# A two-block transformer on one core: the head of the kernel sends and norms its input tile by tile

## The chip, the core and the metric

The kernel runs on one core of a Trainium2 chip. A core has a matrix engine (PE, with its weight loads PEld), a vector engine (DVE), a scalar engine (ACT), a general engine (POOL) and a sequencer for transfers (SP). Each runs its own instruction stream in order, and they wait for one another on semaphores. ACT and POOL can issue transfers too; all transfers of the core share 16 DMA engines. SBUF is the on-chip memory with 128 partitions, PSUM the memory that PE writes to. The metric is the device time of one execution in microseconds (us), the median of several. Everything is computed in float32.

## The reference, cut to what matters

The model is two blocks over one sequence of 512 tokens with 1024 channels. The first block opens with a norm and a projection, and that opening is what the change is about:

```python
def rms_norm(t, g):
    tf = t.astype(jnp.float32)
    y = tf * lax.rsqrt(jnp.mean(tf * tf, axis=-1, keepdims=True) + NORM_EPS)
    return (y * g.astype(jnp.float32)).astype(t.dtype)

h = rms_norm(x, mix_norm_g[l])          # x: 1 x 512 x 1024
u = h @ w_in[l]                         # 1024 x 2816
conv_in = u[..., :2 * CONV_CH]          # 512 columns: gated depthwise convolution, 31 taps
qkv = u[..., 2 * CONV_CH:]              # 2304 columns: 12 heads, rotary embedding, dilated attention
```

After it come the output projection, an attention over a memory of 256 rows, a mixture of 32 experts of which each token uses two, and a second block (attention with forgetting, a state-space scan, another mixture of experts). None of that is changed.

## The kernel before, in words

The program is written out by hand: one function per stage and engine (`stage1_pe`, `stage1_act`, `stage1_dve`, `stage1_pool`, then `attn1_...`, `mem_pe` and so on), and each engine's block calls its own in order. Nothing reorders the work; the order of the calls and the semaphore waits set it. The sequence is held as four tiles of 128 tokens (`T` = 4), the channels as eight pieces of 128 (`KD` = 8). The matrix multiply needs the channels on the partitions, so `hT[:, k, :]` (piece k of the normed input, all 512 tokens) is made by transposing on PE.

The head goes like this. SP issues the whole of `x` (2 MB) as one transfer (L2692), then seven parameter arrays (`cols`, `rows`, `ident`, `mask1`, `tri`, `tokid`, `posi`, L2693 to L2697) that all count on the semaphore `par_in`, then the weights of the projection in chunks of 512 columns (`load_part`, L318), into a ring of four slots. POOL issues the small transfer `wfv` first of all (L2786): eight columns of a matrix that is 4 KB or more per row, so pieces of 32 bytes, not used until the second block.

DVE fills four areas with constants. ACT and DVE then wait for `x` and for all seven parameter arrays (L488 and L489, L541 and L542), PE for the parameters (L2716). ACT sums the squares of the four tiles (L340), one after another. DVE turns the four sums into four variances with one instruction (L353), POOL raises them to the power -0.5 with one (L368), DVE scales the four tiles (L357). PE transposes 32 squares of 128 x 128 (L376), piece by piece: piece k of all four tiles, so that piece 0 is not complete until the last tile is scaled. ACT and DVE take the eight pieces out of PSUM in turn and apply the gain (L348, L364). Then comes a barrier of the three engines, `end_stage` (L236), a drain and a wait for the three others' drains:

```python
            pe.wait_ge(S("par_in"), 16 * 7)          # L2716
            norm_pe("n1", xn_tile, T)                # L434
            end_stage("pe", pe)                      # L436
```

After it PE runs the projection (L255 through `accumulate`): 16 groups of eight matmuls of 128 x 512, in the order of `FT`. The first four groups use chunk `in0`, the next four `in1`, and so on. Group g from 6 on also waits until group g - 6 has been taken out of PSUM (`g1_out`, L446). While PE runs, DVE computes the angles of the rotary embedding (L546 to L549) from `posi`, ACT clears a table in memory with seven transfers (L495), takes the sine and the cosine (L498, L499) and the sigmoid of the gate (L503), and DVE runs the taps of the convolution.

Of the kernel before, what the change touches and what calls it, by code (L numbers as in the profile page):

```python
# [8 lines left out]
P = 128  # L9
# [6 lines left out]
D = 1024  # L16
# [66 lines left out]
def shared_semaphores():  # L83
# [4 lines left out]
    for tag, tiles in (("n1", 4), ("n4", 2), ("nm", 4), ("n5", 0), ("n6", 0), ("n7", 0), ("n9", 0)):  # L88
        names = (("sumsq", tiles), ("var", 1), ("rstd", 1), ("xn", tiles), ("turned", KD))
        if tag == "n4":  # L90
            names = (("sumsq", MT), ("var", 1), ("rstd", 1), ("xn", MT), ("turned", 4))
# [9 lines left out]
    for tag, n in (("a1", HEADS * T), ("n5", 0), ("x5", MEM_HEADS * T), ("n6", 0), ("n7", 0), ("f2", 8 * T), ("n9", 0)):  # L101
        if not n:
            for what, family, m in (("added", "masked", T if tag == "n7" else 2 * T), ("xa", "probs", T),
                                    ("hd", "pT", T), ("ha", "out", 1 if tag == "n7" else T)):
                shared[f"{tag}_{what}"] = (f"attn_{family}", counts.get(family, 0))
                counts[family] = counts.get(family, 0) + m
            continue
# [9 lines left out]
    shared["x5_max"] = ("a1_sq", HEADS // 2)  # L117

# [36 lines left out]
def recycled_semaphores():  # L155
# [8 lines left out]
               "halves_set", "x_in", "mem_in", "sp_ra", "sp_sin", "x5_max", "x5_norm")  # L164
# [8 lines left out]
def build(nc, a, out):  # L173
    es = ExitStack()
    with es:
# [13 lines left out]
        def since(name):  # L189

            return SHARED.get(name, (name, 0))[1]
# [116 lines left out]
        def load_part(sp, part):  # L308
            for i, (nm, w, c0, c1) in enumerate(chunks):
# [177 lines left out]
        def stage1_act(act):  # L487
            act.wait_ge(S("x_in"), 16)  # L488
            act.wait_ge(S("par_in"), 16 * 7)  # L489
            norm_act("n1", x_tile, D, T, hT_tile, gains("mix_g"))  # L490
            end_stage("act", act)
# [5 lines left out]
            act.wait_ge(S("angles"), 1)  # L497
            nc.scalar.activation(sin_t, sin_t, ACT.Sin)  # L498
# [33 lines left out]
        def stage1_dve(dve):  # L532
# [92 lines left out]
        def stage1_pool(pool):  # L625
            pool.wait_ge(S("halves_set"), 1)
            norm_pool("n1", T)
# [377 lines left out]
        def s5_matrices_pool(pool):  # L1005
# [11 lines left out]
            after_stage(pool, 3)  # L1017
# [1054 lines left out]
        STAGES_TO_MOE1 = 2 + 1 + 1 + 2  # L2072
# [34 lines left out]
        def entry_act(act):  # L2107
# [11 lines left out]
            for t in range(T):  # L2119
                act.wait_ge(S(f"xback_{t}"), 16)  # L2120
# [14 lines left out]
        def entry_dve(dve):  # L2135
# [4 lines left out]
            def gained(t):  # L2140
                dve.wait_ge(S(f"xback_{t}"), 16)
                dve.tensor_tensor(x[:, t, :], xn[:, t, :], final_g, ALU.mult).then_inc(S("n7_added"), 1)
# [642 lines left out]
        def _(pool):  # L2785
            pool.dma_start(wfv, a["w_in_2"][0][:, 1536:1544].rearrange("(k p) n -> p k n", p=P)).then_inc(S("wf_in"), 16)  # L2786
# [110 lines left out]
```

## Time and profile before

| | |
|---|---|
| median of 3 runs | 1939.67 us (1931.63 to 1944.18) |
| profiled execution, its own time | 1940.19 us |
| its span | 1938.3 us |
| PE busy | 1657.2 us, 85% of the span |
| DVE, ACT, POOL busy | 503.6, 327.0, 375.5 us |
| chain that ended last | PE 54%, DMA 29%, DVE 6%, POOL 4%, ACT 3% |
| mean granted PE clock of the span | 0.944 of full speed |
| time at which the projection's first matmul starts | 35.50 us |

The page divides the span into 40 slices, so the first slice (48 us) holds the whole head: PE is busy half of it, and DMA moves 285 GB/s. Everything finer has to be asked of the trace: the chain of waits in a window of the first 64 us, the transfers with the time from issue to landing, and the busy time and bytes moved by stretch. Two readings need care. A landing is counted from the issue of a transfer, so it holds the time behind earlier transfers in the queue. And the granted clock of the first stretches is printed as 1.00, though the first change that the trace records comes only when PE has run for some us; a matmul's own duration says more there.

### The profile page before, as it was taken

Reading aid. Unit: us, or ns where it says so; the run is one execution under the profiler, and the core shown is the slowest. Engines: PE = TensorE matmul, PEld = TensorE weight load, DVE = VectorE, ACT = ScalarE, POOL = GpSimd, SP = SyncE. Lnnn points to the kernel's source line nnn. Section 1 sums busy time; section 2 is a strip of 40 time slices with the busy share of each in tenths; the row PEclk is TensorE's granted clock in tenths of the full one; section 3 lists DMA queues with packets and bytes.
Section 4 is the critical chain, followed back from the end, with each engine's and each line's share of the span. In section 5 each row is a group of like instructions: output and inputs, shape, how many; then the busy total and the mean of one; then the engine's idle time right before and its main releaser. Section 6 shows DMA issues by size and latency. Waiting matters only on the chain.

```text
span 1938.3 us, 18659 instructions
## 1 busy us (share of the span) xinstructions
PE 1657.2 (85%) x7098; PEld 809.9 (42%) x7098; DVE 503.6 (26%) x1200; ACT 327.0 (17%) x705; POOL 375.5 (19%) x357
## 2 busy tenths in 40 slices
PE   4999889989897988777787759899999997988775
PEld 2444447434545332322222225545644444544332
DVE  3466666020315210100000021613300015311110
ACT  2001552020412000000000020313400012111111
POOL 0011552974011011111111110010001001232222
PEclk9999999989997999999999969999999997999998
DMA  8112103430653999999999854940031235999992
GB/s 285 65 44 87 66 1 130 160 112 22 226 200 143 412 414 420 419 417 418 417 419 416 314 204 113 256 107 33 1 78 56 84 156 223 402 398 404 402 398 96
DMA packets 101670, 436.96 MB, mean 225 GB/s; under 512 B 15608, under 2 KB 23448, under 8 KB 75344
## 3 DMA queue, kind: packets, MB, share of 16 engines
q1 hardware_dynamic: 59136, 299.22, 40.6%
q10 hardware_dynamic: 23984, 105.80, 13.3%
q0 software_dynamic: 18464, 30.76, 6.0%
q8 instruction: 58, 0.95, 0.2%
q14 instruction: 28, 0.23, 0.0%
HBM read 414.19 MB, written 40.91 MB: 235 GB/s over the span
## 4 chain that ended last, share of the span: by engine, by line
PE 54%; DMA 29%; DVE 6%; POOL 4%; ACT 3%; issue 3%; SPq 1%; ACTq 0%; POOLq 0%; DVEq 0%
PE ps L255 27%; DMA ring<-in_w 18%; PE ps L1711 8%; DMA ring<-in_w_expert_up 7%; PE ps L1294 5%; DMA work<-hmid,rowtok 2%; PE ps L1727 2%; PE ps L2192 2%; PE ps L721 1%; PE ps L706 1%; PE ps L1320 1%; PE ps L680 1%; DMA ring<-in_positions 1%; POOL ring L1054 1%; POOL ring L1055 1%
## 5 line engine op out<-in xcount | busy, mean ns | idle before, releaser
L1711 PE MATMUL ps<-ring,work 128*64 128x256 f32 (+1 forms) x1472 | 273.8, 530 | 75.0 <-DMA ring<-in_w 41.6
L255 PE MATMUL ps<-kept,ring 128*128 128x512 f32 x640 | 280.7, 598 | 2.5 <-DVE kept L1349 1.3
L1711 PEld LDWEIGHTS ps<-ring,work 128*64 128x64 f32 x1472 | 113.2, 150 | 239.4 <-issue 120.1
L255 PEld LDWEIGHTS ps<-kept,ring 128*128 128x128 f32 x640 | 122.2, 192 | 156.6 <-issue 154.0
L1829 DVE TENSOR_TENSOR work<-work,ps 128x256 f32<-128x256 f32 (+1 forms) x64 | 22.7, 355 | 627.5 <-ACT work L1788 606.8
L1727 PE MATMUL ps<-ring,work 128*64 128x512 f32 x544 | 129.3, 610 | 27.2 <-issue 26.2
L1711 PE MATMUL ps<-kept,work 128*64 128x512 f32 (+1 forms) x640 | 120.1, 533 | 28.4 <-DMA kept<-in_w 17.9
L1875 POOL DMA_INDIRECT hres<-work,rowdst x33 | 51.7, 1567 | 433.6 <-ACT work L1798 433.3
L255 PE MATMUL ps<-ring,kept 128*128 128x512 f32 (+1 forms) x320 | 124.7, 550 | 0.3 <-PE ps L255 0.3
L1294 PE MATMUL ps<-ring,kept 128*128 128x512 f32 x256 | 114.8, 603 | 1.7 <-ACTq L239 1.4
L1788 ACT ACTIVATE work<-ps 128x256 f32<-128x256 f32 (+1 forms) x64 | 21.2, 331 | 456.9 <-PE ps L1711 456.9
L1711 PEld LDWEIGHTS ps<-kept,work 128*64 128x64 f32 x640 | 50.2, 150 | 100.5 <-issue 52.8
L1875 POOL DMA_INDIRECT out<-work,rowdst x33 | 51.7, 1568 | 192.5 <-ACT work L1798 191.3
L255 PEld LDWEIGHTS ps<-ring,kept 128*128 128x128 f32 x320 | 60.5, 190 | 62.5 <-issue 60.9
L1798 ACT ACTIVATE work<-ps,gslot 128x512 f32<-128x512 f32 x64 | 44.0, 687 | 244.0 <-PE ps L1727 244.0
L1727 PEld LDWEIGHTS ps<-ring,work 128*64 128x64 f32 x544 | 40.5, 139 | 84.1 <-issue 82.8
L1294 PEld LDWEIGHTS ps<-ring,kept 128*128 128x128 f32 x256 | 48.4, 193 | 61.0 <-issue 58.0
L255 PE MATMUL ps<-work,ring 128*128 128x128 f32 (+2 forms) x416 | 66.7, 310 | 1.5 <-DVEq L239 0.5
L1727 PE MATMUL ps<-kept,work 128*64 128x512 f32 x240 | 55.9, 599 | 11.2 <-issue 11.2
L255 PEld LDWEIGHTS ps<-work,ring 128*128 128x128 f32 x416 | 58.9, 191 | 7.4 <-DVE ring L2596 2.3
L1294 PE MATMUL ps<-ring,work 128*128 128x512 f32 x128 | 56.9, 596 | 2.4 <-POOL work L2681 2.2
L2681 POOL TENSOR_TENSOR work<-work 128x512 f32<-128x512 f32 x8 | 10.1, 1261 | 234.7 <-DVE work L2674 234.7
(449 smaller groups left out, 1877.3 us busy)
## 6 DMA issues: line engine op xcount, KB each, us to landing
ring<-in_w SPq DMA_DIRECT2D x46, 2048.0 KB, 30.3
kept<-in_w SPq DMA_DIRECT2D x21, 2048.0 KB, 30.1
ring<-in_w ACTq DMA_DIRECT2D x20, 2048.0 KB, 22.6
ring<-in_w_in SPq DMA_DIRECT2D x13, 2048.0 KB, 14.8
ring<-in_w_expert_gate SPq DMA_DIRECT2D x24, 1024.0 KB, 33.8
ring<-in_w_expert_up SPq DMA_DIRECT2D x24, 1024.0 KB, 40.5
kept<-in_w ACTq DMA_DIRECT2D x9, 2048.0 KB, 25.6
ring<-in_w_expert_down ACTq DMA_DIRECT2D x18, 1024.0 KB, 29.2
```

Of the source, the lines that this page charges most:

```text
L255: last = nc.tensor.matmul(out_, l, r, start=i == 0, stop=i == len(pairs) - 1)
L680: nc.tensor.matmul(ps[:, (i + m) % 4, :], q1[r, h // 2, t * P:t * P + P], k1[r, h // 2, :], start=True, stop=True).then_inc(S("a1_scores"), 1)
L706: last = nc.tensor.transpose(ps[:, 4 + j % 2, c * P:c * P + P], pr1(j)[:, c * P:c * P + P], ident[:, :])
L721: last = nc.tensor.matmul(ps[64 * m:64 * m + 64, 6, :], v1[:, c, (2 * hp + m) * 64:(2 * hp + m) * 64 + 64], pT1(hp)[:, m, c, :], start=c = ...
L1294: last = nc.tensor.matmul(ps[:, b * T + t, :], src(k)[:, t * P:t * P + P], weight(nm)[:, k, :], start=k == 0, stop=k == KD - 1)
L1711: last = nc.tensor.matmul(ps[64 * hf:64 * hf + 64, bank, 0:ff].rearrange("p (w n) -> p w n", w=2), xT[:, k, :], up[:, :, k * ff + hf * hw: ...
L1727: last = nc.tensor.matmul(ps[64 * hf:64 * hf + 64, bank, :], hT_[:, i % nch, 64 * (i // nch):64 * (i // nch) + 64], down[:, i, hf * 512:hf ...
L1788: nc.scalar.activation(gb[:, i % 2, 0:hw], ps[:, i % 2, 0:hw], ACT.Silu).then_inc(S(f"silu{m}"), 1)
L1798: nc.scalar.activation(yb[:, j % 4, :], ps[:, 6 + j % 2, :], ACT.Identity, scale=gslot[:, expert(j):expert(j) + 1]).then_inc(S(f"yready{m} ...
L1829: dve.tensor_tensor(hb[:, i % 2, 0:hw], gb[:, i % 2, 0:hw], ps[:, i % 2, hw:ff], ALU.mult).then_inc(S(f"hready{m}"), 1)
L1875: return pool.indirect_dma_start(out=by_half(acc(m)), out_offset=bass.IndirectOffsetOnAxis(ap=rows_, axis=0), in_=src, in_offset=None, bou ...
L2192: last = nc.tensor.matmul(ps[64 * q:64 * q + 64, s2, :], hs[:, k, 2 * s2 + q, :], weight("u")[:, k, :], start=k == 0, stop=k == KD - 1)
```

## The change

The diff is cut to what the instructions do. What is left out renumbers barriers (one fewer ahead of every later one) and semaphores that are used again later, and moves no work.

```diff
 block.sync:
-            sp.dma_start(x[:, :, :], a["x"][0].rearrange("(t p) n -> p t n", p=P)).then_inc(S("x_in"), 16)
-            for dst, src in ((cols[:, :], a["cols"]), (rows[:, :], a["rows"].to_broadcast([P, NROW])),
-                             (ident[:, :], a["ident"]), (mask1[:, :], a["mask1"]),
-                             (tri[:, :], a["tri"]), (tokid[:, :], a["tokid"]),
-                             (posi[:, :], a["positions"].unsqueeze(0).to_broadcast([P, SEQ]))):
-                sp.dma_start(dst, src).then_inc(S("par_in"), 16)
+            for t in range(T):
+                sp.dma_start(x[:, t, :], a["x"][0, t * P:t * P + P, :]).then_inc(S(f"x_tile_{t}"), 16)
             load_part(sp, False)
 load_part:
+                if i == 1:
+                    for dst, src in ((posi[:, :], a["positions"].unsqueeze(0).to_broadcast([P, SEQ])),
+                                     (rows[:, :], a["rows"].to_broadcast([P, NROW])), (mask1[:, :], a["mask1"]),
+                                     (tri[:, :], a["tri"]), (tokid[:, :], a["tokid"])):
+                        sp.dma_start(dst, src).then_inc(S("par_in"), 16)
 stage1_pe:
-            norm_pe("n1", xn_tile, T)
-
-            end_stage("pe", pe)
+            for t in range(T):
+                pe.wait_ge(S("n1_xn"), since("n1_xn") + t + 1)
+                for k in range(KD):
+                    last = nc.tensor.transpose(ps[:, 2 * t + k // 4, (k % 4) * P:(k % 4) * P + P],
+                                               xn[:, t, k * P:k * P + P], ident[:, :])
+                last.then_inc(S("n1_turned"), 1)
+            pe.wait_ge(S("n1_hd"), since("n1_hd") + T)
+            pe.wait_ge(S("n1_ha"), since("n1_ha") + T)
 stage1_act:
-            act.wait_ge(S("x_in"), 16)
-            act.wait_ge(S("par_in"), 16 * 7)
-            norm_act("n1", x_tile, D, T, hT_tile, gains("mix_g"))
-            end_stage("act", act)
+            act.dma_start(cols[:, :], a["cols"]).then_inc(S("id_in"), 16)
+            act.dma_start(ident[:, :], a["ident"]).then_inc(S("id_in"), 16)
+            act.wait_ge(S("halves_set"), 1)
+            nc.scalar.activation(nmax[:, 0:16], halves[:, :], ACT.Square)
+            for t in range(T):
+                act.wait_ge(S(f"x_tile_{t}"), 16)
+                if t >= 2:
+                    act.wait_ge(S("n1_sumsq"), since("n1_sumsq") + t - 1)
+                nc.scalar.activation(junk[:, :] if t % 2 else junk2[:, 0:D], x[:, t, :], ACT.Square,
+                                     accum_out=st[:, t:t + 1]).then_inc(S("n1_sumsq"), 1)
+            act.wait_ge(S("id_in"), 32)
+            for t in range(T):
+                act.wait_ge(S("n1_turned"), since("n1_turned") + t + 1)
+                for k in range(4, KD):
+                    last = nc.scalar.activation(hT[:, k, t * P:t * P + P], ps[:, 2 * t + 1, (k - 4) * P:(k - 3) * P],
+                                                ACT.Identity, scale=col("mix_g", k))
+                last.then_inc(S("n1_ha"), 1)
 ...
             act.wait_ge(S("angles"), 1)
+            act.wait_ge(S("par_in"), 16 * 5)
 stage1_dve:
-            dve.wait_ge(S("x_in"), 16)
-            dve.wait_ge(S("par_in"), 16 * 7)
-            norm_dve("n1", x_tile, D, T, xn_tile, hT_tile, gains("mix_g"))
-            end_stage("dve", dve)
-
+            def scaled(t):
+                dve.wait_ge(S(f"x_tile_{t}"), 16)
+                dve.wait_ge(S("n1_sumsq"), since("n1_sumsq") + t + 1)
+                dve.tensor_scalar(st[:, 8 + t:9 + t], st[:, t:t + 1], 1.0 / D, EPS, ALU.mult, ALU.add).then_inc(
+                    S("n1_var"), 1)
+                dve.wait_ge(S("n1_rstd"), since("n1_rstd") + t + 1)
+                dve.tensor_scalar(xn[:, t, :], x[:, t, :], st[:, 16 + t:17 + t], None, ALU.mult).then_inc(S("n1_xn"), 1)
+
+            def turned(t):
+                dve.wait_ge(S("n1_turned"), since("n1_turned") + t + 1)
+                dve.tensor_tensor(hT[:, 0:4, t * P:t * P + P], ps[:, 2 * t, :].rearrange("p (k s) -> p k s", k=4),
+                                  col("mix_g", 0, 4).unsqueeze(2).to_broadcast([P, 4, P]), ALU.mult).then_inc(S("n1_hd"), 1)
+
+            scaled(0)
+            scaled(1)
+            dve.wait_ge(S("id_in"), 32)
+            for t in range(2, T):
+                scaled(t)
+                turned(t - 2)
+            for t in range(T - 2, T):
+                turned(t)
+
+            dve.wait_ge(S("par_in"), 16 * 5)
 stage1_pool and block.gpsimd:
-            pool.dma_start(wfv, ...).then_inc(S("wf_in"), 16)     (was ahead of stage1_pool)
-            norm_pool("n1", T)
+            for t in range(T):
+                pool.wait_ge(S("n1_var"), since("n1_var") + t + 1)
+                nc.gpsimd.tensor_tensor(st[:, 16 + t:17 + t], st[:, 8 + t:9 + t], halves[:, 0:1], ALU.pow).then_inc(
+                    S("n1_rstd"), 1)
+            pool.dma_start(wfv, ...).then_inc(S("wf_in"), 16)
 block.tensor:
-            pe.wait_ge(S("par_in"), 16 * 7)
+            pe.wait_ge(S("id_in"), 32)
             stage1_pe(pe)
+            pe.wait_ge(S("par_in"), 16 * 5)
```

How this moves instructions shows at three places. The first is SP's queue at the start of the program (`kept<-in_x` is the input, `ring<-in_w_in` the chunks of the projection, `ring<-in_mask` the array `mask1`). Before:

```order
L2692 DMA kept<-in_x 128x4x1024
L2697 DMA cols<-in_cols 128x247
L2697 DMA rows<-in_rows 128x844
L2697 DMA ident<-in_ident 128x128
L2697 DMA ring<-in_mask 128x896
L2697 DMA tri<-in_tri 128x128
L2697 DMA tokid<-in_tokid 128x4
L2697 DMA ring<-in_positions 128x512
L318 DMA ring<-in_w_in 128x8x512 x5
```

and with the change:

```order
L2745 DMA kept<-in_x 128x1024 x4
L329 DMA ring<-in_w_in 128x8x512
L325 DMA ring<-in_positions 128x512
L325 DMA rows<-in_rows 128x844
L325 DMA ring<-in_mask 128x896
L325 DMA tri<-in_tri 128x128
L325 DMA tokid<-in_tokid 128x4
L329 DMA ring<-in_w_in 128x8x512 x4
```

The input is four transfers, the first chunk of weights stands ahead of the parameters, and `cols` and `ident` have gone to ACT's queue. The second place is DVE at the same point (`kept` holds `x`, `xn` and `hT`; `st` the sums, variances and factors). Before:

```order
L539 MEMSET work 128x1024
L353 TENSOR_SCALAR st<-st 128x4
L357 TENSOR_SCALAR kept<-kept,st 128x1024 x4
L364 TENSOR_SCALAR kept<-ps,cols 128x512 x4
L546 CAST kept<-ring 128x512
```

and with the change:

```order
L569 MEMSET work 128x1024
L574 TENSOR_SCALAR st<-st 128x1
L577 TENSOR_SCALAR kept<-kept,st 128x1024
L574 TENSOR_SCALAR st<-st 128x1
L577 TENSOR_SCALAR kept<-kept,st 128x1024
L574 TENSOR_SCALAR st<-st 128x1
L577 TENSOR_SCALAR kept<-kept,st 128x1024
L581 TENSOR_TENSOR kept<-ps,cols 128x4x128
L574 TENSOR_SCALAR st<-st 128x1
L577 TENSOR_SCALAR kept<-kept,st 128x1024
L581 TENSOR_TENSOR kept<-ps,cols 128x4x128 x3
L594 CAST kept<-ring 128x512
```

The variance and the scaling now alternate tile by tile, and the first tile is taken out of PSUM before the last is scaled. The third is ACT. Before:

```order
L340 ACT_TABLE_LOAD
L340 ACTIVATE junk,st<-kept 128x1024 x4
L348 ACTIVATE kept<-ps,cols 128x512 x4
L492 DMA kept<-in_perm 128x128
L495 DMA ssm_t<-work 512x1x32
```

and with the change:

```order
L504 DMA cols<-in_cols 128x247
L505 DMA ident<-in_ident 128x128
L507 ACT_TABLE_LOAD
L507 ACTIVATE nmax<-halves 128x16
L512 ACTIVATE ring,st<-kept 128x1024
L512 ACTIVATE junk,st<-kept 128x1024
L512 ACTIVATE ring,st<-kept 128x1024
L512 ACTIVATE junk,st<-kept 128x1024
L518 ACTIVATE kept<-ps,cols 128x128 x16
L521 DMA kept<-in_perm 128x128
```

Two transfers, the table load and a small activation stand ahead of the first square, and sixteen activations of 128 columns take the place of four of 512.

## Rows read from the trace of the kernel before

**Rows 1.** Chain of waits, 0 to 64 us: start, duration (us), what it was.
```profile
4.79 13.91 DMA ring<-in_positions
...
18.78 1.28 ACT L340
...
23.61 1.16 ACT junk L340 x2
...
26.32 2.75 DVE kept L357 x4
...
35.50 27.75 PE ps L255 x64
```

**Rows 2.** Transfers, 0 to 130 us: issuer, count, KB each, us from issue to landing.
```profile
kept<-in_x SPq DMA_DIRECT2D x1, 2048.0 KB, 14.2
...
ring<-in_positions SPq DMA_DIRECT2D x1, 256.0 KB, 13.9
...
kept<-in_perm ACTq DMA_DIRECT2D x1, 64.0 KB, 4.9
...
wf<-in_w_in POOLq DMA_DIRECT2D x1, 32.0 KB, 12.1
```

**Rows 3.** POOL's queue, 5 to 13 us: packets, MB, share of the 16 DMA engines.
```profile
q0 software_dynamic: 30, 0.03, 43.5%
```

**Rows 4.** Timeline of the issuing queues; then landings of the first and second weight chunk.
```profile
1.29 1.12 POOL L2786 DMA_DIRECT2D wf<-in_w_in  x1 [0.87 <-POOLq L2890]
...
7.48 7.92 SPq L318 DMA_DIRECT2D ring<-in_w_in  x2
...
ring<-in_w_in SPq DMA_DIRECT2D x1, 2048.0 KB, 16.6
...
10.18 5.22 SPq L318 DMA_DIRECT2D ring<-in_w_in  x1
ring<-in_w_in SPq DMA_DIRECT2D x1, 2048.0 KB, 19.4
```

**Rows 5.** Busy time by stretch; the last three columns are granted clock, DMA share, GB/s.
```profile
0.00:4.00 4.00, 0.00 (x0) 0.00 (x0) 2.22 (x4) 0.00 (x0) 1.31 (x5) 1.00 0.49 130
4.00:6.00 2.00, 0.00 (x0) 0.00 (x0) 0.75 (x1) 0.00 (x0) 0.00 (x0) 1.00 1.06 417
7.00:13.00 6.00, 0.00 (x0) 0.00 (x0) 0.00 (x0) 0.00 (x0) 0.00 (x0) 1.00 0.55 189
15.00:20.00 5.00, 0.00 (x0) 0.00 (x0) 0.00 (x0) 1.22 (x1) 0.00 (x0) 1.00 1.05 393
```

**Rows 6.** Chain of waits, 420 to 495 us: a later norm, last tile.
```profile
425.97 0.22 DVE st L1434
...
426.26 0.56 POOL st L1399
...
427.76 1.11 PE ps L1320 x8
...
428.89 0.70 DVE kept L1349
...
430.13 30.77 PE ps L255 x64
...
461.04 27.72 PE ps L255 x64
```

**Rows 7.** Chain at 395 to 410 us; two stretches with PE busy, and the clock.
```profile
403.33 1.97 PE ps L1320 x8
...
429.50:436.50 7.00, 6.37 (x8) 2.74 (x9) 0.08 (x1) 0.54 (x3) 6.69 (x6) 0.52 0.33 124
606.00:638.00 32.00, 20.41 (x110) 15.31 (x112) 14.41 (x58) 4.69 (x10) 4.46 (x5) 0.52 0.58 211
```

**Rows 8.** Timeline, 399 to 400 us: POOL and DVE side by side.
```profile
399.49 3.50 POOL L1065 MEMSET ring<- 128x4096 f32 x1
...
399.56 3.71 DVE L1338 TENSOR_SCALAR kept<-kept,st 128x512 f32<-128x512 f32 x1 [3.43 <-POOL st L1399]
```

More of the change, by code:

```diff
@@ L89, in shared_semaphores @@
         names = (("sumsq", tiles), ("var", 1), ("rstd", 1), ("xn", tiles), ("turned", KD))
+        if tag == "n1":
+            names = (("sumsq", T), ("var", T), ("rstd", T), ("xn", T), ("turned", T))
         if tag == "n4":
@@ L100, in shared_semaphores @@
     counts = {}
-    for tag, n in (("a1", HEADS * T), ("n5", 0), ("x5", MEM_HEADS * T), ("n6", 0), ("n7", 0), ("f2", 8 * T), ("n9", 0)):
+    for tag, n in (("n1", 0), ("a1", HEADS * T), ("n5", 0), ("x5", MEM_HEADS * T), ("n6", 0), ("n7", 0), ("f2", 8 * T), ("n9", 0)):
         if not n:
@@ L104, in shared_semaphores @@
                                     ("hd", "pT", T), ("ha", "out", 1 if tag == "n7" else T)):
+                if tag == "n1" and what in ("added", "xa"):
+                    continue
                 shared[f"{tag}_{what}"] = (f"attn_{family}", counts.get(family, 0))
@@ L117, in shared_semaphores @@
     shared["x5_max"] = ("a1_sq", HEADS // 2)
+    for t in range(T):
+        shared[f"xback_{t}"] = (f"x_tile_{t}", 16)
     for family, tags in (("sum", (("g1", 24), ("m4", 12), ("r3", 8), ("q5", 8), ("r5", 8), ("u", 4), ("glu", 4),
@@ L163, in recycled_semaphores @@
                "ctok_in", "ln_done", "ln_sig", "angles", "ln_var", "ln_rstd", "sines", "perm_in", "zeros", "zeroed",
-               "halves_set", "x_in", "mem_in", "sp_ra", "sp_sin", "x5_max", "x5_norm")
+               "halves_set", "id_in", "mem_in", "sp_ra", "sp_sin", "x5_max", "x5_norm")
     assert len(later) == len(earlier)
@@ L626, in stage1_pool @@
             pool.wait_ge(S("halves_set"), 1)
-            norm_pool("n1", T)
+            for t in range(T):
+                pool.wait_ge(S("n1_var"), since("n1_var") + t + 1)
+                nc.gpsimd.tensor_tensor(st[:, 16 + t:17 + t], st[:, 8 + t:9 + t], halves[:, 0:1], ALU.pow).then_inc(
+                    S("n1_rstd"), 1)
+            pool.dma_start(wfv, a["w_in_2"][0][:, 1536:1544].rearrange("(k p) n -> p k n", p=P)).then_inc(S("wf_in"), 16)
             for f in range(12):
@@ L1016, in s5_matrices_pool @@
             halves = (slice(0, 64), slice(64, P))
-            after_stage(pool, 3)
+            after_stage(pool, 2)
             pool.dma_start(raw_bc, a["ssm_bc"]).then_inc(S("bc_in"), 16)
@@ L2069, in over_sp @@
                                      ).then_inc(S(f"over{m}_down_{p}"), 16)
-        STAGES_TO_MOE1 = 2 + 1 + 1 + 2
+        STAGES_TO_MOE1 = 1 + 1 + 1 + 2
         sp_ = lambda at, *shape: (lambda v: v if len(shape) == 1 else v.rearrange("p (a b) -> p a b", a=shape[0]))(
@@ L2119, in entry_act @@
             for t in range(T):
-                act.wait_ge(S(f"xback_{t}"), 16)
+                act.wait_ge(S(f"xback_{t}"), since(f"xback_{t}") + 16)
                 square(t, xn[:, t, :], 2 * t)
@@ L2140, in gained @@
             def gained(t):
-                dve.wait_ge(S(f"xback_{t}"), 16)
+                dve.wait_ge(S(f"xback_{t}"), since(f"xback_{t}") + 16)
                 dve.tensor_tensor(x[:, t, :], xn[:, t, :], final_g, ALU.mult).then_inc(S("n7_added"), 1)
@@ L2691, in _ @@
         def _(sp):
-            sp.dma_start(x[:, :, :], a["x"][0].rearrange("(t p) n -> p t n", p=P)).then_inc(S("x_in"), 16)
-            for dst, src in ((cols[:, :], a["cols"]), (rows[:, :], a["rows"].to_broadcast([P, NROW])),
-                             (ident[:, :], a["ident"]), (mask1[:, :], a["mask1"]),
-                             (tri[:, :], a["tri"]), (tokid[:, :], a["tokid"]),
-                             (posi[:, :], a["positions"].unsqueeze(0).to_broadcast([P, SEQ]))):
-                sp.dma_start(dst, src).then_inc(S("par_in"), 16)
+            for t in range(T):
+                sp.dma_start(x[:, t, :], a["x"][0, t * P:t * P + P, :]).then_inc(S(f"x_tile_{t}"), 16)
             load_part(sp, False)
@@ L2785, in _ @@
         def _(pool):
-            pool.dma_start(wfv, a["w_in_2"][0][:, 1536:1544].rearrange("(k p) n -> p k n", p=P)).then_inc(S("wf_in"), 16)
             stage1_pool(pool)
```

## The prediction

> **What bounds the kernel now.** I began with the chain of waits over the first 64 us, because the change touches nothing behind it. The reader is to see two halves in [rows 1]. Up to 18.7 us nothing is computed on the path: all engines wait for `posi`, the last of the transfers issued ahead of the weights. From 18.78 to 35.50 us a chain of 16.7 us follows that PE mostly only ends: table load, four squares of 1.16 us, variance, power, four scalings in 2.75 us, 32 transposes, two evictions, barrier. At 35.50 PE starts on 64 matmuls without a gap, and the same chain stays on PE from there through the projection. So the head is worth 35.50 us, and what the change can save is what it takes off that number, if PE finds its weights and runs as fast as now.
>
> Next the transfers. Input and parameters are only 3.3 MB, 8 to 9 us at the rate of 393 to 417 GB/s that the steady stretches show [rows 5], yet `x` lands at 0.72 + 14.2 = 14.9 us and `posi` at 4.79 + 13.9 = 18.7 us [rows 2]. Between them lies a stretch of 6 us at 189 GB/s in which the engines are charged only 0.55 of their time [rows 5]. The row that stands out beside it is POOL's queue: 0.03 MB that hold 43.5% of 16 engines over 8 us, 3.5 us on each engine [rows 3]. That is `wfv`, 32-byte pieces, issued at 1.29 us and landed 12.1 us later [rows 2, 4]. I read the slow stretch as its doing: `x` is being sent at 417 GB/s until it comes [rows 5], and finishes only after it.
>
> The Trainium skill, page "DMA: Bandwidth & Descriptors", section "Queues, rings and completion order", says that a DMA engine takes turns between queues packet by packet and finishes a packet before it switches. By that rule every packet of `x` behind a slow one of `wfv` waits for it whole, and moving `wfv` frees `x`; the trace agrees in the 3.5 us per engine [rows 3].
>
> **The change, part by part.** 1. *First tile.* 130 GB/s over 4 us is 0.52 MB, exactly one tile, by 4.0 us [rows 5]. `cols` and `ident` (0.19 MB) now run on ACT's queue beside it, 0.45 us at 417 GB/s, and the landing follows the last byte: I take 4.8 us. Upper end: the 64 KB of `perm` took 4.9 us beside a full stream [rows 2]; with that from an issue at 0.72, and 1.1 us for the other 0.46 MB, 6.7 us. Lower end 4.0.
>
> The same page, section "Anatomy of one DMA — SWDGE (gpsimd) path", gives a fixed cost of about 2.0 us per transfer and 436 GB/s; an estimate from it is 0.72 + 2.0 + 1.2 = 3.9 us for the first tile. By that estimate the sum would be 0.9 us better; no row here shows such a transfer alone.
>
> 2. *The chain per tile.* A later norm of this kernel is already built tile by tile and gives the prices: variance 0.22 us, power of one column 0.56, 0.07 between the two [rows 6]. The scaling is 2.75 / 4 = 0.69 [rows 1]. With the gaps that is 1.6 us per tile, all in series on DVE, which waits for POOL in between. First square done at 4.8 + 1.16, seen by DVE at 6.1. Three tiles: 10.9. Then one eviction, 0.70 [rows 6]: 11.6. Fourth tile: 13.2. Its eight transposes: 1.97 us at half clock, against 1.11 at full [rows 6, 7]: 15.2. From the start of the last DVE eviction to PE's first matmul the later norm takes 430.13 - 428.89 = 1.24 us, ACT's four small activations included [rows 6]: **16.5 us**. The other two evictions of DVE fit under the transposes.
>
> 3. *Covers.* ACT's four squares end at 4.8 + 4 x 1.2 = 9.6, before DVE wants the last at 11.6; the table load (1.28 us [rows 1]) now lies ahead of the first tile. The last tile needs 2.29 MB: 0.52 by 4.0, the rest in 4.2 us, so 8.2, landed about 8.9; it is wanted at 10.3. Without that cover every us later is a us lost. `cols` and `ident` are wanted at 9.3 and come by about 1.7 + 4.9 = 6.6. The first weights: 4.39 MB, 0.52 by 4.0 and 3.87 at 393 GB/s, so 13.9, landed about 14.6, 2 us before PE wants them.
>
> 4. *Barrier removed.* It stood between the last eviction and PE; in the 1.24 there is none, so nothing is added.
>
> 5. *PE's clock.* In the old head the first 64 matmuls took 27.75 us, as long as 64 in a settled stretch (27.72): the transposes had run in one block before them [rows 1, 6]. Now the transposes come in four bursts with gaps. The nearest row is the later norm, also in bursts: its next 64 matmuls took 30.77, **3.05 us** more, with a granted clock of 0.52, that is 1.2 GHz, over 429.5 to 436.5 [rows 6, 7]. I charge that; the other end is nothing.
>
> 6. *`wfv` moved.* POOL issues it after the fourth power, about 12.6 us, beside DVE's last scaling. Where POOL filled memory beside a scaling, that scaling took 3.71 us instead of 0.69 [rows 8]. The issue takes 1.12 us [rows 4], so 0 to 1.1 us; I take 0, the middle of what the two rows allow being well under the other terms. The transfer itself now runs into the second weight chunk. PE wants that one half of 27.75 after its start, plus the slow clock: 33 us. It landed at 10.18 + 19.4 = 29.6 us [rows 4] with the same bytes and `wfv` ahead of it. ACT's clearing of memory (1.8 MB, 4.6 us at 393) now comes early enough to push it at worst to 34. I charge nothing; the end is 1 us.
>
> 7. *Parameters behind the weights.* 1.2 MB more in the queue behind 13.9 us, so landed at about 18, 1.5 us after PE's start. DVE's angles, ACT's sine and sigmoid hang on them; PE asks for the sigmoid first in group 6, 6 x 27.75 / 8 = 20.8 us after its start, and in the old head never waited for it, since its 64 matmuls ran through [rows 1]. Nothing; if the slack there was under 1.5 us, the rest of it.
>
> Sum: 35.5 - 16.5 = 19.0 saved at the start of PE, less 3.05, is 15.95. From there on every wait is on PE or on a transfer that PE's progress releases, so the shift should reach the end whole. The profiled execution was 1940.19 us, 0.5 above the median: 1924.2, which I give as **1924 us**.
>
> **Rivals.** *A, the input still comes late.* If the slow stretch is not the doing of `wfv` but of so many transfers at once, the last tile lands at 14.9. Then 1.16 + 0.15 for the square, 1.6 for the chain, 1.97 and 1.24: PE at 21.0, saving 14.5 - 3.05 = 11.4, 1928.8 us. For it: engines idle in that stretch, which blocked packets alone do not explain. Against it: the 417 GB/s before. Chance 0.17.
>
> *B, PE keeps full clock.* Nothing is lost at the start: 1921.2 us. For it: 32 transposes in 8 us are PE work too. Against it: [rows 7]. Chance 0.20.
>
> *C, the clock stays low.* With PE busy 64% of 606 to 638 us the granted clock was 0.52 throughout [rows 7]. If the bursts leave PE at 1.2 GHz into the projection, each us at that level loses half of it: the change decides to the bad from 2 x 19.0 = 38 us at half clock. All first 64 matmuls so would take 55.5 us, a loss of 27.75: 1949 us. Against it: busy without gaps, PE came back within 7 us in [rows 6, 7]. Chance 0.03.
>
> *D, the shift is lost on the way.* Some later stage starts by something that PE does not set, and the end stays: 1938 to 1941 us. For it: DMA has 29% of the whole chain. Against it: every such load waits for a slot that PE frees. Chance 0.08.
>
> The forecast has 0.52. **Numbers.** The runs before spread over 12.6 us, so a median of a few is good to some 4 us; 1% is 19.4 us and about what can be told from no change. Faster by over 1% means below 1920.3: near half of B, a fifth of the forecast for noise and for unpriced luck: 0.24. Slower by over 1%: C beyond its point and what nobody thought of: 0.03. Within: 0.73. The range must hold 8 in 10: the forecast's own is 1919 to 1930 (terms 1, 5, 6 and noise); it takes in A and B with noise: 1915 to 1932.
>
> **What the profile after would show.** The first matmul of 128x512 at 16 to 18 us (A: 21). Landings of the four tiles at about 5, 6, 8, 9. POOL's powers at 0.56 each. The first 64 matmuls at 30 to 31 us (B: under 28). No wait of PE for a weight chunk in the first 200 us. The attention's start earlier by as much as the projection's. Wrong would be: DVE waiting for `cols`, PE waiting for chunk two, or a power of 1.05 us per tile instead of 0.56, which would cost 4 x 0.5 = 2 us.

## The result and the profile after

The changed kernel takes 1912.93 us (median of 4, 1910.08 to 1920.20), the kernel before 1936.47 (median of 4, the three shown and one more). The ratio is 0.9882, 95% interval 0.9856 to 0.9908: faster by 1.2%. The forecast was 1924 us with a range of 1915 to 1932: the direction is right, and the time lies 2 us below the range. The profiled execution took 1914.55 us, 25.64 less than the one of before; the part of this that the head explains is 20.3 us, as shown below.

The chain of waits over the first 64 us of the changed kernel, in the columns of [rows 1]:

```profile
0.72 4.07 DMA kept<-in_x
...
4.81 1.16 ACT ring L512 x2
...
6.08 0.17 DVE st L574
...
6.39 0.58 POOL st L677
...
7.00 0.76 DVE kept L577
...
7.90 4.92 PE ps L448 x24
...
12.84 1.76 ACT kept L518 x6
...
15.21 27.72 PE ps L261 x64
```

What PE waited for last is in its row of the timeline:

```profile
15.21 9.25 PE L261 MATMUL ps<-kept,ring 128*128 128x512 f32 x21 [1.28 <-ACT kept L518]
```

It is ACT's four small activations for the last tile, which end at 15.1 us; DVE's last eviction ends at 14.7.

The first tile is there at 4.79 us, PE transposes from 7.90, and the first 128x512 matmul is at 15.21 instead of 35.50. The 64 matmuls take 27.72 us, as before (27.75), and end at 42.93 instead of 63.25: 20.3 us earlier. The stretch that was slow before [rows 3, 5] is gone:

```profile
7.00:13.00 6.00, 5.06 (x25) 4.86 (x26) 4.01 (x9) 5.11 (x15) 2.65 (x4) 1.00 1.04 395
```

395 GB/s where it was 189, and PE, DVE and ACT are busy in it. The transfers, in the columns of [rows 2] (the first row is the fourth tile, issued at 2.10 us, the second the first chunk of weights, issued at 2.72):

```profile
kept<-in_x SPq DMA_DIRECT2D x1, 512.0 KB, 6.8
ring<-in_w_in SPq DMA_DIRECT2D x1, 2048.0 KB, 11.6
cols<-in_cols ACTq DMA_DIRECT2D x1, 123.5 KB, 4.3
wf<-in_w_in POOLq DMA_DIRECT2D x1, 32.0 KB, 13.0
```

So the last tile lands at 8.9 us and the first chunk at 14.3, close to what was worked out (8.9 and 14.6). The chunk is now 0.9 us ahead of PE and no more.

Behind the head the two profiles drift apart by 5 us. The starts of some groups of PE in both, from the trace:

| PE's group | before, us | after, us | earlier by |
|---|---|---|---|
| first scores of the attention (L680, now L732) | 201.2 | 181.0 | 20.2 |
| transposes of the memory (L689, now L741) | 293.0 | 272.7 | 20.3 |
| projection behind the memory (L1294, now L1346) | 359.3 | 340.6 | 18.7 |
| router of the first block (L1286, now L1338) | 589.3 | 568.2 | 21.1 |
| state-space part (L2340, now L2392) | 1234.9 | 1213.3 | 21.6 |
| last matmul of the last experts (L1727, now L1779) | 1923.6 | 1897.9 | 25.7 |

It goes down as well as up. The granted clock is at half for 215.2 us in all in the one trace and for 200.7 in the other, added up from the clock's records within the span (the expectation below has both 1.6 us higher). Up to the router of the first block the steps stand where one execution has such a stretch and the other has not. The twelve profiles of this study that run the whole computation show it: from the first scores to the transposes of the memory they take 91.7 to 92.0 us where 6.8 us of it are at half, 88.9 or 89.0 where none are, and 93.2 in the one with 10.2. From there to the projection it is 67.9 or 68.0 us with 3.4 us at half and 66.2 or 66.3 with none. The last step, 4.1 us in the last stretch of the table, is not explained in this way. That stretch takes 684.3 to 688.9 us over the twelve profiles, in no clear order with its time at half clock, and the cause of the step stays open.

### The profile page after: what moved, and what is told of

Read it like the earlier page. It is cut to its first block, busy times and chain, and to the rows that moved or that the text cites. A ratio compares the mean times of both kernels' runs of the same rounds, so it can differ in the third digit from the quotient of the medians.

```text
span 1912.7 us, 18683 instructions
## 1 busy us (share of the span) xinstructions
PE 1652.7 (86%) x7098; PEld 807.8 (42%) x7098; DVE 503.5 (26%) x1203; ACT 328.6 (17%) x718; POOL 376.9 (20%) x360
## 3 DMA queue, kind: packets, MB, share of 16 engines
q10 hardware_dynamic: 24272, 105.99, 13.5%
## 4 chain that ended last, share of the span: by engine, by line
PE 53%; DMA 30%; DVE 7%; POOL 4%; ACT 3%; issue 2%; SPq 1%; ACTq 0%; POOLq 0%; DVEq 0%
PE ps L261 27%; DMA ring<-in_w 19%; DMA ring<-in_w_expert_up 9%; PE ps L1763 8%; PE ps L1346 5%; PE ps L1779 2%; PE ps L2244 2%; DMA work<-hmid,rowtok 1%; PE ps L773 1%; PE ps L758 1%; SPq L1942 1%; PE ps L1372 1%; PE ps L732 1%; POOL ring L1106 1%; POOL ring L1107 1%
## 5 line engine op out<-in xcount | busy, mean ns | idle before, releaser
L1779 PE MATMUL ps<-ring,work 128*64 128x512 f32 x544 | 129.5, 611 | 27.2 <-issue 26.2
L1346 PE MATMUL ps<-ring,kept 128*128 128x512 f32 x256 | 114.5, 602 | 1.7 <-ACTq L245 1.4
L1840 ACT ACTIVATE work<-ps 128x256 f32<-128x256 f32 (+1 forms) x64 | 21.1, 330 | 458.4 <-PE ps L1763 458.4
L1779 PEld LDWEIGHTS ps<-ring,work 128*64 128x64 f32 x544 | 40.5, 139 | 84.1 <-issue 82.7
L1346 PEld LDWEIGHTS ps<-ring,kept 128*128 128x128 f32 x256 | 48.2, 193 | 60.9 <-issue 57.8
L1779 PE MATMUL ps<-kept,work 128*64 128x512 f32 x240 | 55.9, 599 | 11.2 <-issue 11.2
L1346 PE MATMUL ps<-ring,work 128*128 128x512 f32 x128 | 56.9, 596 | 2.4 <-POOL work L2733 2.2
L2733 POOL TENSOR_TENSOR work<-work 128x512 f32<-128x512 f32 x8 | 10.1, 1261 | 234.7 <-DVE work L2726 234.7
## 6 DMA issues: line engine op xcount, KB each, us to landing
kept<-in_w ACTq DMA_DIRECT2D x9, 2048.0 KB, 25.6
```

What stands on the lines that cost most here:

```text
L1346: last = nc.tensor.matmul(ps[:, b * T + t, :], src(k)[:, t * P:t * P + P], weight(nm)[:, k, :], start=k == 0, stop=k == KD - 1)
L1779: last = nc.tensor.matmul(ps[64 * hf:64 * hf + 64, bank, :], hT_[:, i % nch, 64 * (i // nch):64 * (i // nch) + 64], down[:, i, hf * 512:hf ...
L1840: nc.scalar.activation(gb[:, i % 2, 0:hw], ps[:, i % 2, 0:hw], ACT.Silu).then_inc(S(f"silu{m}"), 1)
```

## The experiments

Ratios are to runs of the kernel before on the same chip, made in the same session. "The end of the 64" is the end of the first 64 matmuls of the projection: it holds both when PE starts and how fast it runs, and it is 63.25 us in the profile of before and 42.93 in the changed one.

### The same kernels again

The changed kernel with no edit:

> The changed kernel once more, timed against the one before in five rounds. Theory 'head plus luck': in the two profiles PE starts the projection 20.3 us earlier and the end comes 25.6 us earlier; the last 5 us arise later, at places where PE's granted clock is at half in one execution and not in the other (216.8 us at half clock before, 202.3 after). Then a new profile again has its first 128x512 matmul at 15.2 us to within 0.2, but another span, and the span goes with the granted clock; over more runs the difference of the medians falls towards 20 us (ratio 0.9895). Rival 'the later stages gain too': the difference stays at 23.5 us or more and the new profile shows the same steps at the same places as the first.

Measured: 0.9906, interval 0.9888 to 0.9924, median 1917.85 of 6 runs, against 1936.51 for 17 runs of before. Its profile:

```profile
0.72 4.25 DMA kept<-in_x
...
13.03 1.11 PE ps L448 x8
...
15.39 27.72 PE ps L261 x64
```

The head repeats within 0.2 us (15.39 against 15.21). The later steps do not: PE starts the projection behind the memory at 336.3 us, 23.0 earlier than in the first profile of before, where the first changed profile had 18.7. So the rival, the same steps at the same places, fell for this part. Its six runs reach from 1912.62 us at a mean granted clock of 0.946 to 1921.89 at 0.942, while the profiled run of 1913.1 us has 0.950. 0.9906 of 1936.5 is a saving of 18.2 us, with 14.7 to 21.7 in the interval; the head's 20.3 lies inside, the 25.6 of the first pair of profiles does not.

The kernel before with no edit:

> The kernel before against itself, for the spread that the executions have of their own and for a second profile of it. Theory: the head repeats to within 0.3 us (first 128x512 matmul at 35.5), while the span differs by some us, with the sum of the stretches at half clock; the ratio is 1.000 with an interval of about 0.2% to each side. Rival: the span repeats to within 1 us, and then the 5 us that the changed kernel's profile gained behind the head were no chance.

Measured: 1.000, interval 0.9986 to 1.0015, median 1936.99. Its ten runs reach from 1930.62 us (clock 0.950) to 1940.48 (clock 0.943). The head does not repeat as closely as I expected: the chain has

```profile
4.31 14.83 DMA ring<-in_positions
...
36.49 23.87 PE ps L255 x55
```

one us later than in the first profile, since the parameters land at 19.1 us instead of 18.7 and the transposes take 6.08 us instead of 5.52. Medians of before over four sets of runs were 1936.5, 1936.5, 1934.3 and 1936.6; the 1939.67 of the section ahead of the prediction was 3 us high, and the 1940.19 from which the forecast was counted 3.7 us.

### The transfer of 32-byte pieces

The changed kernel with `wfv` first again:

```diff
 stage1_pool:
-            pool.dma_start(wfv, ...).then_inc(S("wf_in"), 16)
 block.gpsimd:
+            pool.dma_start(wfv, ...).then_inc(S("wf_in"), 16)
             stage1_pool(pool)
```

> The changed kernel with one line moved back: POOL issues the transfer of 32-byte pieces (wfv) first of all. Theory: its slow packets fall among those of x again; between about 7 and 13 us the rate drops from 395 GB/s to about 200, the last tile lands at 12 to 15 us instead of 8.9, PE starts the projection at 18 to 21 us instead of 15.2, and the run is 3 to 6 us slower than the changed kernel. Rival (A of the prediction): the slow stretch came from many small transfers at once, which are no longer ahead; then x lands by 9 us as now, and nothing moves by more than 1 us.

Measured: 0.9939, interval 0.9919 to 0.9959, so 8 us slower than the changed kernel by the medians (1925.98 against 1917.85), more than expected. In its chain, its stretches and POOL's queue at 5 to 13 us:

```profile
1.63 14.48 DMA kept<-in_x
...
21.12 1.98 PE ps L448 x8
...
24.36 29.74 PE ps L261 x64
```

```profile
7.00:13.00 6.00, 3.64 (x16) 3.28 (x16) 1.54 (x3) 0.43 (x2) 0.55 (x1) 1.00 0.47 174
15.00:28.70 13.70, 8.27 (x22) 5.08 (x23) 6.91 (x14) 6.62 (x20) 1.10 (x2) 0.51 1.02 375
```

```profile
q0 software_dynamic: 28, 0.03, 50.5%
```

The rate falls to 174 GB/s, the third tile lands at 16.1 us, the fourth at 17.2, and PE starts 9.2 us later. It also starts slower: 29.74 us for the 64 and a clock of 0.51 over 15.0 to 28.7. (The DMA engines are busy for 0.47 of the slow stretch, and for 0.55 of it in the kernel before; why they stand idle for the rest stays open.) The end of the 64 is at 54.10, 11.2 us later. One transfer of 32 KB costs half of what the whole change gains.

The kernel before with this line alone moved, behind the power of the norm:

```diff
 block.gpsimd:
-            pool.dma_start(wfv, ...).then_inc(S("wf_in"), 16)
 stage1_pool:
             norm_pool("n1", T)
+            pool.dma_start(wfv, ...).then_inc(S("wf_in"), 16)
```

> The kernel before with the same one line moved only: wfv is issued behind the power, at about 26 us. Theory: no slow stretch at 7 to 13 us; x, parameters (3.3 MB) land by 10 to 12 us instead of 18.7, all later steps of the head follow unchanged (16.7 us), PE starts at 27 to 29 us instead of 35.5, and the time falls by 7 to 8 us. Rival: the parameters themselves are slow to send (512-byte to 3.5 KB rows, eight transfers); they still land at 16 us or later and the time falls by under 3 us.

Measured: 0.9967, interval 0.9954 to 0.9980, a saving of 6.4 us (3.9 to 8.9).

```profile
4.49 9.04 DMA ring<-in_positions
...
24.26 6.16 PE ps L376 x29
...
31.28 27.75 PE ps L255 x64
```

```profile
kept<-in_x SPq DMA_DIRECT2D x1, 2048.0 KB, 7.9
```

`x` lands at 8.6 us instead of 14.9, `posi` at 13.5 instead of 18.7, and PE starts 4.2 us earlier, at 31.28 and not at the 27 to 29 expected. Neither theory holds whole: the slow stretch was the doing of `wfv`, but the parameters took longer than their bytes (13.5 where I had 10 to 12; 319 GB/s over 10 to 13.5 us). And of the 5.2 us by which they land earlier PE keeps 4.2, since the four scalings take 3.07 us here instead of 2.75 and the transposes 6.16 instead of 5.52.

Is it the pieces, or that POOL issues a transfer there? The changed kernel with POOL sending `cols` first, rows of 988 bytes:

```diff
 stage1_act:
-            act.dma_start(cols[:, :], a["cols"]).then_inc(S("id_in"), 16)
 block.gpsimd:
+            pool.dma_start(cols[:, :], a["cols"]).then_inc(S("cols_in"), 16)
             stage1_pool(pool)
 ...
```

The dots stand for the waits of ACT, DVE and PE, which go over to `cols_in`.

> The changed kernel, with POOL sending the array cols (rows of 988 bytes, 124 KB) first of all instead of ACT; wfv stays behind the powers. It asks what of wfv slowed x: its pieces of 32 bytes, or that POOL issued a transfer at this time. Theory: the pieces; the rate at 7 to 13 us stays near 395 GB/s, x lands by 9 us, and PE starts at 15 to 16 us unless cols itself lands after 9 us. Rival: POOL's queue; the rate falls to about 200 GB/s and x lands at 12 us or later.

Measured: one run, 1913.46 us. One stretch, the landing of `cols`, and the chain:

```profile
7.00:13.00 6.00, 4.63 (x28) 4.42 (x29) 4.01 (x9) 5.37 (x17) 2.92 (x4) 1.00 1.04 390
```

```profile
cols<-in_cols POOLq DMA_DIRECT2D x1, 123.5 KB, 5.2
```

```profile
14.94 27.72 PE ps L261 x64
```

Four times the bytes from the same queue at the same moment, and 390 GB/s. So it is not that POOL issues a transfer there but how that transfer is cut: 1024 pieces of 32 bytes, spread over the rows of a matrix, against 128 rows of 988. Which of these, size, number or spacing, does it is not told apart.

### The order of the transfers, and the norm by tiles

The parameters ahead of the first chunk of weights:

```diff
-                if i == 1:
+                if i == 0:
                     for dst, src in ((posi[:, :], ...), (rows[:, :], ...), ...
```

> The changed kernel with the five parameter arrays sent ahead of the first chunk of weights instead of behind it. Theory: 1.2 MB ahead of the chunk at 390 to 400 GB/s are 3 us, so the chunk lands at 17 to 17.5 us instead of 14.3 and PE, ready at 15.2, starts 2 us later. Rival: small rows are sent more slowly than their bytes say; the chunk lands at 19 us or later.

Measured: one run, 1924.69 us.

```profile
5.29 14.62 DMA ring<-in_w_in
20.05 29.64 PE ps L261 x64
```

The chunk lands at 19.9 us, 5.6 later and not 3, and PE starts at 20.05. After its wait the 64 matmuls take 29.64 us. Two stretches and POOL's queue at 13 to 20 us say where the other 2.6 us went:

```profile
7.00:10.00 3.00, 2.10 (x10) 2.13 (x11) 1.67 (x5) 2.69 (x6) 1.10 (x2) 1.00 1.04 330
...
16.00:20.00 4.00, 0.00 (x0) 0.00 (x0) 3.78 (x7) 0.00 (x0) 0.00 (x0) 0.64 1.24 278
```

```profile
q0 software_dynamic: 27, 0.03, 25.7%
```

The parameters go at 330 GB/s instead of 393 to 417, and behind them the chunk, now late, meets `wfv`, which holds 1.8 us of every engine there.

`x` as one transfer:

```diff
-            for t in range(T):
-                sp.dma_start(x[:, t, :], a["x"][0, t * P:t * P + P, :]).then_inc(S(f"x_tile_{t}"), 16)
+            sp.dma_start(x[:, :, :], a["x"][0].rearrange("(t p) n -> p t n", p=P)).then_inc(S("x_tile_0"), 16)
 ...
```

(The dots: ACT and DVE wait for `x_tile_0` alone.)

> The changed kernel with x as one transfer of 2 MB instead of four; all engines wait for the whole of it. Theory: it lands at 8 to 9 us (the last tile lands at 8.9 now), the four squares follow at 1.2 us each, the last one's variance, power, scaling, transposes and evictions take 4.5 us more, and PE starts at 17.5 to 18 us, 2.5 us later than the changed kernel. Rival: four transfers cost the queue something that one does not; x lands by 7.5 us and the loss is under 1.5 us.

Measured: one run, 1917.11 us.

```profile
0.72 8.39 DMA kept<-in_x
...
19.54 27.72 PE ps L261 x64
```

It lands at 9.1 us, where the four tiles are done at 8.9, so four transfers cost the queue nothing. PE starts at 19.54, 4.3 later and not 2.5: all four steps of DVE and POOL now run behind the landing at 1.5 us each, and not only the last.

The changed transfers with the norm of before in one piece, and no barrier:

```diff
 stage1_dve:
+            dve.tensor_scalar(st[:, 8:8 + T], st[:, 0:T], 1.0 / D, EPS, ALU.mult, ALU.add).then_inc(S("n1_var"), 1)
+            dve.wait_ge(S("n1_rstd"), since("n1_rstd") + 1)
+            for t in range(T):
+                dve.tensor_scalar(xn[:, t, :], x[:, t, :], st[:, 16 + t:17 + t], None, ALU.mult).then_inc(S("n1_xn"), 1)
+ ...
+            for k in range(1, KD, 2):
+                dve.wait_ge(S("n1_turned"), since("n1_turned") + k + 1)
+                dve.tensor_scalar(hT[:, k, :], ps[:, k, :], col("mix_g", k), None, ALU.mult).then_inc(S("n1_hd"), 1)
```

> The changed kernel's transfers, table load and missing barrier, but the norm itself as before: one variance for four tiles, one power, four scalings, transposes piece by piece, evictions piece by piece. Theory: the tile-wise chain is a part of the gain of its own. The four squares still end at 10.1 us; from there the old chain took 35.50 - 24.77 = 10.7 us with the barrier, so PE starts the projection at 20.5 to 21 us, 5.5 us later than the changed kernel, with its 64 matmuls at 27.7 us, and the time is 5 to 6 us above the changed kernel's. Rival: the transfers are the whole gain and the order of the norm is covered by the landing of the first weights (14.3 us); then PE starts by 17 us.

Measured: 0.9945, interval 0.9928 to 0.9962, median 1922.46 of 7 runs.

```profile
2.10 6.86 DMA kept<-in_x
...
8.98 1.16 ACT junk L507 x2
...
10.49 1.06 POOL st L379
11.58 3.07 DVE kept L582 x4
14.70 5.21 PE ps L387 x29
19.93 0.76 DVE kept L586
20.74 27.75 PE ps L261 x64
```

PE starts at 20.74, as expected: the norm by tiles is worth 5.5 us of the 20.3, and the transfers, the table load and the missing barrier together the other 14.8. The two chains say how that divides: what all wait for lands at 8.96 us instead of 18.70, which is 9.7 us; one square stands behind it instead of the table load and four squares, 4.9 us; and from the last square to PE it takes 10.6 us against 10.7, so the barrier was worth next to nothing (0.05 us between DVE's last eviction and PE, where the kernel before has 0.08).

DVE scaling the last tile ahead of the first eviction:

```diff
-            for t in range(2, T):
-                scaled(t)
-                turned(t - 2)
-            for t in range(T - 2, T):
-                turned(t)
+            scaled(2)
+            scaled(3)
+            for t in range(T):
+                turned(t)
```

> The changed kernel with DVE scaling the last tile ahead of the first eviction. DVE's eviction of tile 0 (0.68 us) stands in the way of the last variance, whose square is there 1.1 us earlier. Theory: the last scaling ends 0.6 us earlier and PE starts the projection at 14.6 to 14.9 us instead of 15.2. Rival: the evictions pile up behind it, or the first weights (landed at 14.3 us) set the start; 15.0 us or later.

Measured: one run, 1917.65 us.

```profile
11.64 2.21 ACT kept L518 x8
14.36 0.53 ACT kept L518 x2
14.98 27.72 PE ps L261 x64
```

It gains 0.23 us, not 0.6: what PE waits for last are ACT's evictions, here as in the changed kernel, and an earlier scaling on DVE helps those little. It is no version to prefer, since a quarter of a us cannot be told from none. No kernel of this study is measurably faster than the changed one.

### PE's clock at the start of the projection

24 of the 32 transposes left out. The evictions of those three tiles read `x` itself instead (behind the dots), so ACT and DVE have the same work; what follows the head works on other data, and only the head is read:

```diff
 stage1_pe:
                 pe.wait_ge(S("n1_xn"), since("n1_xn") + t + 1)
+                if t < T - 1:
+                    pe.sem_inc(S("n1_turned"), 1)
+                    continue
                 for k in range(KD):
 ...
```

> Part of the computation changes: the transposes of tiles 0 to 2 are left out, PE only signals, and their evictions read x untransposed; all else stands, so DVE and ACT do the same work and PE has 8 transposes ahead of the projection instead of 32. What follows has other data (another routing), so only the head is read. Theory on the clock: what PE did in the 7 us ahead of the first matmul decides; with 8 transposes the first 64 matmuls of 128x512 take 30 to 31 us, with a granted clock at half for some us after about 15 us, where with 32 they took 27.7. Rival: the clock at the start has nothing to do with the transposes (it is up at that time anyway); the 64 matmuls take 27.7 us again.

Measured, in the head of one profile:

```profile
12.74 1.98 PE ps L451 x8
...
15.99 29.36 PE ps L261 x64
```

With PE idle until 12.74 the eight transposes take 1.98 us, where the changed kernel's last eight take 1.11, and the 64 matmuls 29.36 where they take 27.72. The trace's first record of the clock, a rise to full, is at 19.30 us; up to it the matmuls start 0.85 us apart, which is 1.2 GHz, and behind it 0.43. In the changed kernel that record is at 12.21 us, among the transposes: they start 0.21 us apart before it and 0.11 after. So the transposes are what brings the clock up in time, and the theory holds; the price is 1.6 us, below the 2.3 to 3.3 that I expected.

How soon the clock rises differs between executions. In six profiles with these 32 transposes ahead the record comes at 10.48, 11.02, 11.87, 12.21, 13.68 and 13.77 us, each time before PE could start the projection (14.94 us at the earliest).

PE made to wait ahead of the projection:

```diff
             pe.wait_ge(S("n1_ha"), since("n1_ha") + T)
+            pe.wait_ge(S("par_in"), 16 * 5)
             used = 0
```

> The changed kernel, but PE waits ahead of the projection for the five parameter arrays, which land at 22.9 us, so that it stands idle for 9 us after its 32 transposes. Theory on the clock: the idle time costs again what the transposes gained; PE starts at 23.0 us and the first 64 matmuls take 29.5 to 31 us, so they end 9.5 to 11 us later than in the changed kernel, and the time is that much longer, since nothing later makes up for it. Rival on the shift: later stages absorb a part; the time grows by under 7 us. Rival on the clock: 27.7 us again.

Measured: 0.9958, interval 0.9941 to 0.9976, median 1927.85 of 5 runs, 10 us above the changed kernel's 1917.85 (made in another session; by the two ratios it is 10.1).

```profile
7.32 15.10 DMA tokid<-in_tokid
22.66 30.08 PE ps L261 x64
```

```profile
22.66 2.90 PE L261 MATMUL ps<-kept,ring 128*128 128x512 f32 x3 [8.14 <-DMA tokid<-in_tokid]
```

```profile
14.00:22.50 8.50, 0.52 (x5) 0.28 (x3) 0.90 (x3) 1.70 (x7) 0.00 (x0) 0.69 1.07 292
22.60:29.00 6.40, 6.33 (x10) 2.79 (x11) 5.65 (x11) 0.00 (x0) 0.00 (x0) 0.62 1.04 380
```

In 8.1 us of idleness the granted clock fell from full to half, at 17.18 us (0.69 on the mean of the first stretch), and it stood at half when the matmuls came: 30.08 us. The end of the 64 is 9.8 us later, and 10 us is what the time lost.

### The end of the 64 against the whole time

| kernel | PE starts | the 64 take | they end | saving if all else stays | measured saving, with interval |
|---|---|---|---|---|---|
| only `wfv` moved | 31.28 | 27.75 | 59.03 | 4.2 | 6.4 (3.9 to 8.9) |
| `wfv` first | 24.36 | 29.74 | 54.10 | 9.2 | 11.8 (7.9 to 15.7) |
| late start | 22.66 | 30.08 | 52.74 | 10.5 | 8.1 (4.6 to 11.4) |
| norm in one piece | 20.74 | 27.75 | 48.49 | 14.8 | 10.6 (7.4 to 13.9) |
| the change | 15.21 | 27.72 | 42.93 | 20.3 | 22.9 (17.8 to 27.9) |
| the change again | 15.39 | 27.72 | 43.11 | 20.1 | 18.2 (14.7 to 21.7) |

Savings are (1 - ratio) x 1936.5, and the fifth column is counted from the 63.25 us of the first profile of before; from the second (64.24) each would be 1.0 higher, and the late start's then just outside its interval. Five of six intervals hold the head's own figure; the norm in one piece falls short by 1 us beyond its interval, and whether a later stage or chance took that stays open.

## Why the prediction was wrong, step by step

- **First tile at 4.8 us (step 1): right**, 4.79. The estimate from the fixed cost in the Trainium skill, page "DMA: Bandwidth & Descriptors", section "Anatomy of one DMA — SWDGE (gpsimd) path", was 3.9, and the trace decides for 4.79. Landings of the last tile and the first chunk: right, 8.9 and 14.3.
- **The chain per tile (step 2): 1.3 us too long.** I had PE at 16.5; it starts at 15.21. A round of variance, power and scaling took 1.5 us where I had 1.6, since the next variance starts while the scaling still ends (7.66 against 7.76), and the last eight transposes ran at full clock, 1.11 us instead of 1.97. The last link was ACT's evictions and not DVE's; it is luck that the stretch from the last transposes to PE still took 1.26 us where I had 1.24.
- **The clock (step 5): this is the step that failed.** It charged 3.05 us for a slow start, from the later norm [rows 6]; the charge was nothing, and with the 0.9 us of the last transposes it makes 3.9 of the 4.4 us by which the head did better than the sum (20.3 against 15.95). The row was the nearest in form and not in what happened to the clock. There the clock was at full and fell at 429.5 us, and PE was busy for 1.4 of the six us ahead of its matmuls. Here it began at half and had to rise, and PE ran 24 transposes, 4.92 us, from 7.90 to 12.82, without a gap, because at half clock it starts the next tile when the last is not yet done; the clock rose among them, at 12.21 us. I had called that "four bursts with gaps" without working out that 24 transposes at 0.2 us fill the three rounds of 1.5 us. Without them the charge is real: 29.36, 29.64, 29.74 and 30.08 us in four experiments. In three PE had done little just before: nothing for 5.65 and 8.14 us (the parameters first, the late start), or nothing up to the last eight transposes. In the fourth, with `wfv` first, it stood for 7.5 us and then ran sixteen transposes in 4.05, and yet the clock rose only at 28.44; why so late stays open. The Trainium skill, page "TensorE: Matmul & The Clock Gate", Part 1, says that the clock is low by default and that activity releases it; these runs agree.
- **`wfv` (the reading of the profile, step 6): right**, and worth more than I gave it: put back, it costs 9 us of PE's start and a slow start besides. Rival A fell with it. The rule of the Trainium skill, page "DMA: Bandwidth & Descriptors", section "Queues, rings and completion order", that an engine finishes a packet before it changes queues fits: 28 slow packets hold half of 16 engines' time over 8 us, while 124 KB in longer rows from the same queue hold up nothing. That it is the packet and not another thing about small pieces no run here shows. Beside DVE's last scaling the issue (11.95, 1.34 us) did no harm: that scaling took 0.75 us like the others.
- **Covers (steps 3, 6, 7): they held.** PE asks for the second chunk at 29.0 us, and its landing is printed as 8.52 + 21.8 = 30.3, yet no matmul of the 64 is late. So the landing column is off there by over a us, and how much slack is left it does not say. The last of the parameters, `tokid`, landed at 22.8 us and not at about 18; DVE stood until then, and PE's 64 matmuls ran through all the same.
- **Barrier removed (step 4): right**, nothing.
- **The shift reaches the end whole: right** within what can be measured, by the table above. Rivals C and D fell; rival B, full clock, is what happened, at a start 1.3 us earlier than it assumed.
- **The base and the noise.** From 1936.5, on which three of the four medians of before agree, 20.3 off gives 1916.2 us, inside the range that I gave. I set out from 1940.19, the one profiled execution. The first four runs of the changed kernel then fell 3.3 us below 1916.2 and the next six 1.7 above; the median of all ten is 1916.0. The range ended 9 us below the forecast, and three errors went the same way: 4.4 us in the head, 3.7 in the base and 3.3 that was chance.

Faster by over 1% had 0.24, within 1% 0.73. The first interval (0.9856 to 0.9908) lies mostly on the faster side of that line and the second (0.9888 to 0.9924) mostly on the other; by the median of all ten runs the change saves 1.06%.

## What to carry to other kernels

Ask of a small transfer how many pieces it is cut into and what is queued beside it. Here 32 KB in pieces of 32 bytes, not used until the second block, held up the input of the whole kernel, and its row in the table of queues showed it. Before charging PE for a cold start, add up what PE does ahead of it, tile by tile, and compare that with the row the price comes from, and ask whether the clock rises or falls in that row. And take the base from as many runs as there are: a median of three was 3 us off where the whole gain was 20.

## What the hardware showed

- Moving one transfer of 32 KB behind the norm gave 6.4 us (3.9 to 8.9) by itself; ahead of everything it cut the rate from 395 to 174 GB/s for 6 us.
- The parameter arrays, rows of 16 bytes to 3.5 KB, went at 319 to 330 GB/s where 4 KB rows of `x` went at 411 to 417.
- In every profile the first work of PE ran at half clock, 1.2 GHz (transposes 0.21 us apart). In six profiles with the changed kernel's 32 transposes ahead the clock rose at 10.48 to 13.77 us, and where nothing then held PE up the 64 matmuls took 27.7 us; with eight transposes it rose at 19.30, and they took 29.36.
- The time of the same kernel differs by 10 us between executions, and only in part with the mean granted clock: 0.950 at 1930.62 us and 0.943 at 1940.48 in one set, but 0.952 at 1937.34 and 0.947 at 1942.29 in another. The head repeats within 1 us. For a change in one place the times at that place are ten times as sharp as the total.
